# Token rows gathered as half rows into both partition halves, and turned by identity products in opposite corners of the array

## The chip, the cores and the metric

The kernel runs on one core of one Trainium2 chip. Its time is the device time of one execution in microseconds (us). The core has five engines that run on their own and wait for each other by semaphores: TensorE (PE in the rows; PEld is its weight loads), VectorE (DVE), ScalarE (ACT), GpSimd (POOL) and SyncE (SP). Transfers between device memory (HBM) and on-chip memory (SBUF) are issued by SP, ACT and POOL and carried by the core's 16 DMA engines. TensorE writes its products to PSUM.

## What is computed

One inference step of a two-layer decoder trunk on 520 token rows of 1024 fp32 values (512 of a prompt, 8 single-token samples). Layer 0 mixes with a gated short convolution, layer 1 with an RG-LRU recurrence. Each mixer is followed by a LayerNorm, a mixture of experts, and a second LayerNorm. Only the mixture of experts matters here:

```python
def hier_moe(x, w_group, w_expert, w_gate, w_up, w_down):   # 4 groups x 8 experts
    g = argmax(x2 @ w_group)                  # one group for each token
    vals, idx = lax.top_k(ep, TOP_K)          # two experts of the 8 in that group
    ...
    def expert_block(args):                   # xb: the rows of the tokens of expert e
        xb, e = args
        hmid = jax.nn.silu(xb @ w_gate[e]) * (xb @ w_up[e])     # 1024 -> 512
        return hmid @ w_down[e]                                 # 512 -> 1024
    ...
    y = jax.ops.segment_sum(y_rows, tok_s, num_segments=t)
```

Each of the 32 experts has three weight matrices of 2 MB in fp32, so a layer reads 201 MB of expert weights, and 520 tokens with two experts each give 32.5 rows for an expert on average.

## The kernel before

**Stages.** Mixer of layer 0, its LayerNorm and routing (0 to 279 us of the profiled execution), experts of layer 0 (to about 780), second LayerNorm and the mixer of layer 1, its norm and routing (to 1041), experts of layer 1 (to about 1548), last norm and output.

**Weights.** `ring` has nine slots of 16 KB in each partition, and each weight matrix of an expert takes one slot. SP issues their transfers in order (`expert`, L352 to L357), each after a wait on `freed` (`room`) until TensorE has used the matrix that was in the slot nine units before. The first three experts of a layer are loaded during the mixer. TensorE releases slots in this order: the down matrix of the last expert with the first product of the next expert, the gate matrix with the last product of `project(0)`, the up matrix with the first instruction of `turn_rows`.

**Rows of an expert.** LayerNorm's rows lie in HBM (`x1_dram`, 520 rows of 4 KB). DVE works out which token stands in which of an expert's 48 places and writes these numbers to `idx` (L1335); GpSimd gathers them with one indirect DMA (`gather`, L480 to L488) into `xg[e % 3]`, a buffer of 48 used partitions by 1024 values. Places without a token are out of bounds and move nothing. Three gathers are issued at once, each later one when TensorE has turned the rows that lay in its buffer (`t_mm`).

**Turning.** Products need the 1024 features on the partitions, so TensorE turns the rows (`turn_rows`, L772 to L778): eight transposes of 64 rows by 128 features into one PSUM bank. DVE scales and shifts them into `xgT` (`turned_rows`, L1388 to L1393).

**An expert** on TensorE (`expert`, L812 to L830): `project(0)` and `project(1)` are the gate and up products, each in two 64-column halves of the array; behind them stands `turn_rows` for the next expert, then `turn_hidden` when DVE has written the hidden values (L1396), then `down`. In the first expert of a layer `overflow_rows` (L761) stands between `turn_rows` and `turn_hidden`: with its result DVE writes the places of the output rows (L1379 to L1385) before it comes to the hidden values. Output rows go back to HBM by two indirect DMAs of half rows each (`scatter`, L492), from partitions 0 to 47 and 64 to 111.

**Ahead of the first expert** TensorE runs 12 products for warming (`warm(WARM)`, L571) while the first rows are gathered, then waits on `gath` and turns them.

Of the kernel before, what the change touches and what calls it, by code (L numbers as in the profile page):

```python
# [7 lines left out]
I32 = mybir.dt.int32  # L8
ALU = mybir.AluOpType
# [4 lines left out]
D = 1024  # L14
# [3 lines left out]
T = SEQ + DEC  # L18
TT = 104
NT = T // TT  # L20
# [10 lines left out]
NE = GROUPS * EPG  # L31
# [4 lines left out]
ROWS = 64  # L36
CAP = 48
OVER = T * TOPK // CAP
# [65 lines left out]
def build(nc, a, outs):  # L104
    y_prompt, y_sample, na_p, na_s, nb_p, nb_s, nh_p, nh_s = outs
    with ExitStack() as ctx:
        def sb(name, shape, dt=F32):
            return ctx.enter_context(nc.sbuf_tensor(name, shape, dt))
# [9 lines left out]
        rows_dram = nc.dram_tensor("yrows", [T, TOPK, D], F32).ap()  # L118
        half_rows = rows_dram.rearrange("t k (h n) -> (t k h) n", h=2)
# [24 lines left out]
        idx = sb("idx", [CAP, NBLK], I32)  # L144
        cur = sb("cur", [CAP, 3], I32)
# [68 lines left out]
        xg = [A[:ROWS, i * D:(i + 1) * D] for i in range(UNROLL)]  # L214
# [224 lines left out]
        def _(pool):  # L439
# [25 lines left out]
            pool.iota(tokid[:, :], pattern=[[TT, NT]], base=-NOROW, channel_multiplier=1,  # L465
# [8 lines left out]
            for l in L:  # L474
# [6 lines left out]
                def gather(e):  # L481
                    if e >= UNROLL:
                        pool.wait_ge(t_mm[l], e - UNROLL + 1)
                    pool.indirect_dma_start(  # L484
                        out=xg[e % UNROLL][:CAP], out_offset=None, in_=x1_dram[l],
                        in_offset=bass.IndirectOffsetOnAxis(ap=idx[:, e:e + 1], axis=0),
                        bounds_check=T - 1, oob_is_err=False,
                    ).then_inc(gath[UNROLL * l + e % UNROLL], 16)  # L488
# [9 lines left out]
                for e in range(NE + UNROLL + 1):  # L498
                    if e < NE:
                        gather(e)  # L500
                    if e == UNROLL + 1:
                        pool.wait_ge(idx_ok[l], 2)
                    if e > UNROLL:
                        d = e - UNROLL - 1
                        pool.wait_ge(y_act[l], d + 1)
                        scatter(yo[d % UNROLL], lambda nh: dest[:, nh, d:d + 1], y_out[d % UNROLL])
                n_over = pool.value_load(over_i[0:1, OVER:OVER + 1], min_val=0, max_val=OVER)
                with pool.If(n_over > 0):
                    pool.wait_ge(t_mm[l], NE)

                    def settle(j):

                        pool.tensor_tensor(unused[:, 2 * l + j:2 * l + j + 1], half_neg[:, :1], half_neg[:, :1],
                                           ALU.mult).then_inc(v_cur[l], 1)

                    with pool.Fori(0, n_over) as o:
                        pool.tensor_copy(cur[:, 0:1], idx[:, bass.ds(o + NE, 1)]).then_inc(v_cur[l], 1)
                        pool.tensor_copy(cur[:, 1:2], dest[:, 0, bass.ds(o + NE, 1)]).then_inc(v_cur[l], 1)
                        pool.tensor_copy(cur[:, 2:3], dest[:, 1, bass.ds(o + NE, 1)]).then_inc(v_cur[l], 1)
                        pool.wait_ge(v_cur[l], o * 5 + 3)  # L520
                        settle(0)
                        pool.indirect_dma_start(
                            out=xg[0][:CAP], out_offset=None, in_=x1_dram[l],
                            in_offset=bass.IndirectOffsetOnAxis(ap=cur[:, 0:1], axis=0),
                            bounds_check=T - 1, oob_is_err=False,
                        ).then_inc(v_gath[l], 16)
                        pool.wait_ge(v_ya[l], o + 1)
                        settle(1)
                        scatter(yo[0], lambda nh: cur[:, 1 + nh:2 + nh], v_out[l])
                        pool.wait_ge(v_out[l], o * 32 + 32)  # L530
                    pool.wait_ge(over_done[l], 1)
# [11 lines left out]
        def _(pe):  # L543
# [93 lines left out]
            for l in L:  # L637
# [134 lines left out]
                def turn_rows(x, done, free=False):  # L772
                    xv = x.rearrange("r (p k) -> r k p", k=KT)
                    for k in range(KT):
                        mm = pe.transpose(ps[:, 0, k * ROWS:(k + 1) * ROWS], xv[:, k, :], ident[:ROWS, :ROWS])  # L775
                        if free and k == 0:
                            mm.then_inc(freed, 1)
                    mm.then_inc(done, 1)  # L778
# [30 lines left out]
                def expert(e, e0, trip=0, more=True, first=False):  # L809
# [8 lines left out]
                    if more:  # L818
                        pe.wait_ge(gath[UNROLL * l + b], 16 * ((e0 + 1) // UNROLL + 1) + trip * 16)
# [13 lines left out]
                pe.wait_ge(gath[UNROLL * l], 16)  # L833
# [10 lines left out]
                with pe.If(n_over > 0):  # L844
# [4 lines left out]
                    with pe.Fori(0, n_over) as o:  # L849
                        pe.wait_ge(v_gath[l], o * 16 + 16)  # L850
# [239 lines left out]
        def _(dve):  # L1090
# [89 lines left out]
            for l in L:  # L1180
# [154 lines left out]
                tsc(idx[:, :NE], ps[:CAP, 5, :NE], float(NOROW), ALU.add).then_inc(idx_ok[l], 1)  # L1335
# [22 lines left out]
                def overflow():  # L1358
# [158 lines left out]
```

## Time and profile before

| | |
|---|---|
| Time, median of three runs | 1599.68 us (1595.18 to 1599.91) |
| Profiled execution, its own time | 1603.98 us |
| Its span | 1601.9 us |
| Mean granted TensorE clock | 0.943 |
| TensorE matmul busy | 1300.0 us (81%) |
| DVE, ACT, POOL busy | 395.9, 202.2, 205.9 us |
| HBM read and written | 459.53 MB, 19.19 MB |

Busy time of TensorE is no bound by itself, since the ends of its pipelined products are modelled. The stretches matter more: in the expert stages the DMA engines are busy nearly all the time; in the mixers they are not. The time outside the span is 2.1 us.

### The profile page before, as it was taken

The numbers are of one execution on the slowest core, as the hardware profiler recorded it, in microseconds if no ns is written. First come the engines' busy times: TensorE is split into PE (matmuls) and PEld (weight loads), VectorE is DVE, ScalarE is ACT, GpSimd is POOL, SyncE is SP. The second block draws the span as 40 slices with busy tenths as digits, with TensorE's granted clock in tenths as the row PEclk, the third lists the DMA queues.
The fourth block names the chain that finished last, engine by engine and source line by source line (L and its number), as shares of the span: only waits on it lengthen the run. The fifth ranks groups of instructions, "written<-read, shape, count | busy, mean of one in ns | idle before, by whom it ended". The sixth has DMA issues, their size and how long they took to land.

```text
span 1601.9 us, 19565 instructions
## 1 busy us (share of the span) xinstructions
PE 1300.0 (81%) x8158; PEld 884.9 (55%) x8158; DVE 395.9 (25%) x809; ACT 202.2 (13%) x318; POOL 205.9 (13%) x228
## 2 busy tenths in 40 slices
PE   8999998999777787778369999799887787777850
PEld 7888876565444444444158887656444444444420
DVE  1211214431111111111145663443111111111116
ACT  1000011000000000000044652200000000000002
POOL 0000001122111111111010000112211111111104
PEclk8999998899999999999779999889999999999985
DMA  9922204799999999999793202469999999999954
GB/s 236 303 105 105 106 1 167 257 399 403 404 409 409 399 410 405 410 399 407 240 293 150 82 29 102 163 252 375 403 406 397 406 412 392 412 395 401 417 182 119
DMA packets 109162, 471.18 MB, mean 294 GB/s; under 512 B 14391, under 2 KB 49207, under 8 KB 91684
## 3 DMA queue, kind: packets, MB, share of 16 engines
q1 hardware_dynamic: 93324, 443.09, 72.2%
q0 software_dynamic: 10240, 17.06, 3.2%
q10 hardware_dynamic: 5552, 10.39, 2.3%
q8 instruction: 32, 0.52, 0.1%
q14 instruction: 14, 0.11, 0.0%
HBM read 459.53 MB, written 19.19 MB: 299 GB/s over the span
## 4 chain that ended last, share of the span: by engine, by line
PE 40%; DMA 29%; SPq 24%; DVE 3%; issue 2%; POOL 1%; ACT 1%; POOLq 0%; DVEq 0%; ACTq 0%
SPq L357 23%; PE ps L547 18%; DMA ring<-in_moe_w_gate 14%; PE ps L785 8%; PE ps L631 7%; DMA ring<-in_moe_w_up 6%; DMA ring<-in_moe_w_down 4%; PE ps L804 4%; DMA Bt<-yrows 1%; DMA ring<-yrows 1%; DMA ring<-in_a_w_in 1%; PE ps L775 1%; PE ps L649 1%; PE ps L683 1%; PE ps L571 1%
## 5 line engine op out<-in xcount | busy, mean ns | idle before, releaser
L785 PE MATMUL ps<-ring,A 128*64 128x256 f32 x4096 | 487.5, 393 | 144.7 <-DMA ring<-in_moe_w_up 97.2
L785 PEld LDWEIGHTS ps<-ring,A 128*64 128x64 f32 x4096 | 320.4, 142 | 332.8 <-issue 135.6
L547 PE MATMUL ps<-A,ring 128*128 128x260 f32 x1280 | 286.2, 386 | 2.5 <-DMA ring<-in_a_w_in 2.5
L804 PE MATMUL ps<-ring,C 128*64 128x512 f32 x1024 | 239.1, 609 | 40.1 <-DMA ring<-in_moe_w_down 15.8
L547 PEld LDWEIGHTS ps<-A,ring 128*128 128x128 f32 x1280 | 245.6, 192 | 41.0 <-issue 2.7
L1396 DVE TENSOR_TENSOR C<-C,ps 128x256 f32<-128x256 f32 x64 | 26.9, 420 | 769.9 <-ACT C L1017 769.9
L804 PEld LDWEIGHTS ps<-ring,C 128*64 128x64 f32 x1024 | 79.1, 139 | 159.3 <-issue 137.7
L484 POOL DMA_INDIRECT A<-x,idx x64 | 61.2, 957 | 487.1 <-PE ps L775 458.3
L631 PE MATMUL ps<-Bt,ring 128*128 128x260 f32 x512 | 116.1, 385 | 1.0 <-ACT C L942 0.8
L631 PEld LDWEIGHTS ps<-Bt,ring 128*128 128x128 f32 x512 | 96.1, 190 | 20.1 <-DVE A L1244 2.5
L1017 ACT ACTIVATE C<-ps 128x256 f32<-128x256 f32 x64 | 24.6, 384 | 569.3 <-PE ps L785 569.2
L775 PEld LDWEIGHTS ps<-ident,A 64*128 64x128 f32 x512 | 61.2, 200 | 24.1 <-issue 23.8
L775 PE MATMUL ps<-ident,A 64*128 64x64 f32 x512 | 70.0, 277 | 0.0
L476 POOL TENSOR_TENSOR stat<-stat,half_neg 104x5 f32<-104x5 f32 x2 | 2.4, 1188 | 462.3 <-DVE stat L1100 462.3
L492 POOL DMA_INDIRECT yrows<-A,Bt x44 | 39.4, 895 | 141.0 <-ACT A L1022 127.7
L492 POOL DMA_INDIRECT yrows<-Bt x44 | 39.9, 907 | 133.2 <-ACT Bt L1022 126.5
L492 POOL DMA_INDIRECT yrows<-C,Bt x40 | 37.4, 934 | 109.6 <-ACT C L1022 103.5
L1393 DVE TENSOR_TENSOR A<-A,gb 128x512 f32<-128x512 f32 x64 | 44.3, 692 | 2.2
L1390 DVE TENSOR_TENSOR A<-ps,gb 128x512 f32<-128x512 f32 x64 | 43.5, 680 | 3.5 <-PE ps L775 3.5
L563 PE MATMUL ps<-ident,C 104*128 104x104 f32 x80 | 13.8, 347 | 36.0 <-ACT C L1056 33.6
L1399 DVE COPY C<-ps 128x256 f32<-128x256 f32 x64 | 27.2, 424 | 36.8 <-PE ps L794 36.8
L1244 DVE SCALAR_TENSOR_TENSOR A<-A,ps 128x520 f32<-128x520 f32 x16 | 11.1, 696 | 90.4 <-PE ps L631 90.4
(210 smaller groups left out, 662.2 us busy)
## 6 DMA issues: line engine op xcount, KB each, us to landing
ring<-in_moe_w_gate SPq DMA_DIRECT2D x64, 2048.0 KB
ring<-in_moe_w_up SPq DMA_DIRECT2D x64, 2048.0 KB
ring<-in_moe_w_down SPq DMA_DIRECT2D x64, 2048.0 KB
ring<-in_a_w_in SPq DMA_DIRECT2D x24, 512.0 KB, 17.8
ring<-in_b_w_in SPq DMA_DIRECT2D x8, 1024.0 KB
ring<-yrows SPq DMA_DIRECT2D x8, 832.0 KB
x<-C ACTq DMA_DIRECT2D x10, 416.0 KB
ring<-in_a_w_out SPq DMA_DIRECT2D x2, 2048.0 KB
```

The costliest lines, as they stand in the source:

```text
L357: sp.dma_start(out, w[l][e]).then_inc(loaded[s], 16)
L484: pool.indirect_dma_start(out=xg[e % UNROLL][:CAP], out_offset=None, in_=x1_dram[l], in_offset=bass.IndirectOffsetOnAxis(ap=idx[:, e:e + 1 ...
L492: pool.indirect_dma_start(out=half_rows, out_offset=bass.IndirectOffsetOnAxis(ap=where(nh), axis=0), in_=rows[nh * ROWS:nh * ROWS + CAP, : ...
L547: mm = pe.matmul(bank, lhs(k), rhs(k), start=(k == 0), stop=(k == KT - 1))
L631: mm = pe.matmul(ps[:, 2 * PAIR[m] + hf, :HALF], ring[:, s, col:col + P], hT[:, k, hf * HALF:(hf + 1) * HALF], start=(k == 0), stop=(k == ...
L775: mm = pe.transpose(ps[:, 0, k * ROWS:(k + 1) * ROWS], xv[:, k, :], ident[:ROWS, :ROWS])
L785: mm = pe.matmul(ps[hf * ROWS:(hf + 1) * ROWS, 1, u * FH:(u + 1) * FH], xgT[:, k, :], ring[:, slot, col:col + FH], start=(k == 0), stop=(k ...
L804: mm = pe.matmul(ps[nh * ROWS:(nh + 1) * ROWS, 2, :], hidT[:, at:at + ROWS], ring[:, slot, m * D + nh * 512:m * D + (nh + 1) * 512], start ...
L1390: tt(xgT, ps[:, 0, :KT * ROWS].rearrange("p (k t) -> p k t", k=KT), gb[:, 2 * l, :].unsqueeze(2).broadcast_to([P, KT, ROWS]), ALU.mult).th ...
L1393: tt(xgT, xgT, gb[:, 2 * l + 1, :].unsqueeze(2).broadcast_to([P, KT, ROWS]), ALU.add).then_inc(ready, 1)
L1396: tt(gated, gated, ps[:, 1, FH:2 * FH], ALU.mult).then_inc(ready, 1)
L1399: dve.tensor_copy(hidT, ps[:, 4, :FT * ROWS]).then_inc(ready, 1)
```

## The change

`xg[i]` becomes 128 partitions by 512 values: partition 0 to 47 hold features 0 to 511 of the 48 places, partition 64 to 111 features 512 to 1023. `gather` issues two indirect DMAs of 48 half rows (2 KB) from `half_x1`, the same rows seen as 1040 half rows, with indices `2t` and `2t + 1`. DVE writes both sets of indices, which now lie in `A` instead of a buffer of their own. `turn_rows` makes sixteen ordinary products with a 64 by 64 identity instead of eight transposes: eight with rows 0 to 63 and columns 0 to 63 of the array, eight with rows 64 to 127 and columns 64 to 127, taking turns, all into PSUM bank 0. The waits on `gath` count 32 for a gather instead of 16. The same is done in the overflow loops, which run only if an expert has more than 48 rows.

```diff
-        xg = [A[:ROWS, i * D:(i + 1) * D] for i in range(UNROLL)]
+        half_x1 = [x.rearrange("t (h n) -> (t h) n", h=2) for x in x1_dram]
+        xg = [A[:, i * 512:(i + 1) * 512] for i in range(UNROLL)]
+        idx = A[:CAP, UNROLL * 512:UNROLL * 512 + 2 * NBLK].bitcast(I32).rearrange("p (h b) -> p h b", h=2)
...
-                def gather(e):
-                    if e >= UNROLL:
-                        pool.wait_ge(t_mm[l], e - UNROLL + 1)
-                    pool.indirect_dma_start(
-                        out=xg[e % UNROLL][:CAP], out_offset=None, in_=x1_dram[l],
-                        in_offset=bass.IndirectOffsetOnAxis(ap=idx[:, e:e + 1], axis=0),
-                        bounds_check=T - 1, oob_is_err=False,
-                    ).then_inc(gath[UNROLL * l + e % UNROLL], 16)
+                def gather(rows, where, done):
+                    for h in range(2):
+                        pool.indirect_dma_start(
+                            out=rows[h * ROWS:h * ROWS + CAP, :], out_offset=None, in_=half_x1[l],
+                            in_offset=bass.IndirectOffsetOnAxis(ap=where(h), axis=0),
+                            bounds_check=2 * T - 1, oob_is_err=False,
+                        ).then_inc(done, 16)
...
                     for k in range(KT):
-                        mm = pe.transpose(ps[:, 0, k * ROWS:(k + 1) * ROWS], xv[:, k, :], ident[:ROWS, :ROWS])
-                        if free and k == 0:
-                            mm.then_inc(freed, 1)
+                        for h in range(2):
+                            r = slice(h * ROWS, (h + 1) * ROWS)
+                            mm = pe.matmul(ps[r, 0, k * ROWS:(k + 1) * ROWS], xv[r, k, :], ident[r, r], start=True, stop=True)
+                            if free and k == 0 and h == 0:
+                                mm.then_inc(freed, 1)
...
-                tsc(idx[:, :NE], ps[:CAP, 5, :NE], float(NOROW), ALU.add).then_inc(idx_ok[l], 1)
+                for h in range(2):
+                    ins = tsc(idx[:, h, :NE], ps[:CAP, 5, :NE], float(NOROW + h), ALU.add)
+                ins.then_inc(idx_ok[l], 1)
...
-                    tsc(idx[:, NE:], ps[:CAP, 5, 128:128 + OVER], float(NOROW), ALU.add)
                     for nh in range(2):
+                        tsc(idx[:, nh, NE:], ps[:CAP, 5, 128:128 + OVER], float(NOROW + nh), ALU.add)
```

On GpSimd, at the start of layer 0's experts (`A<-x_0` is a gather, `yrows<-` a scatter), these stood before:

```order
L484 DMA A<-x_0,idx 48x1024 [waits idx_ok0,turned1,x1_out]
L484 DMA A<-x_0,idx 48x1024 x2
L484 DMA A<-x_0,idx 48x1024 [waits t_mm0] x2
L492 DMA yrows<-A,Bt 2080x512 [waits y_act0,idx_ok0]
L492 DMA yrows<-A,Bt 2080x512
```

and these stand there now:

```order
L484 DMA A<-x_0,A 48x512 [waits idx_ok0,turned1,x1_out]
L484 DMA A<-x_0,A 48x512 x5
L484 DMA A<-x_0,A 48x512 [waits t_mm0]
L484 DMA A<-x_0,A 48x512
L484 DMA A<-x_0,A 48x512 [waits t_mm0]
L484 DMA A<-x_0,A 48x512
L492 DMA yrows<-A,Bt 2080x512 [waits y_act0,idx_ok0]
```

Each gather is two DMAs in a row, and nothing else changed its place.

On TensorE, from the warming products to the first overflow product of layer 0, these stood before:

```order
L571 MATMUL ps<-ident 128x128 x12
L775 MATMUL ps<-ident,A 128x64 [waits gath0_0]
L775 MATMUL ps<-ident,A 128x64 x7
L785 MATMUL ps<-ring,A 64x256 [waits loaded1,t_sb0]
L785 MATMUL ps<-ring,A 64x256 x15
L785 MATMUL ps<-ring,A 64x256 [waits gath0_1,loaded2]
L785 MATMUL ps<-ring,A 64x256 x15
L775 MATMUL ps<-ident,A 128x64 x8
L761 MATMUL ps<-Bt 48x32 [waits hot_ok]
```

and these stand there now:

```order
L569 MATMUL ps<-ident 128x128 x12
L775 MATMUL ps<-ident,A 64x64 [waits gath0_0]
L775 MATMUL ps<-ident,A 64x64 x15
L785 MATMUL ps<-ring,A 64x256 [waits loaded1,t_sb0]
L785 MATMUL ps<-ring,A 64x256 x15
L785 MATMUL ps<-ring,A 64x256 [waits gath0_1,loaded2]
L785 MATMUL ps<-ring,A 64x256 x15
L775 MATMUL ps<-ident,A 64x64 x16
L759 MATMUL ps<-Bt 48x32 [waits hot_ok]
```

Eight transposes with 128 output partitions have become sixteen products with 64, at the same two places. An ordinary fp32 product in such a list can be two instructions in the trace.

## Rows read from the trace of the kernel before

**Rows 1.** The page: what the DMA engines moved, in 40 slices of the span.
```profile
GB/s 236 303 105 105 106 1 167 257 399 403 404 409 409 399 410 405 410 399 407 240 293 150 82 29 102 163 252 375 403 406 397 406 412 392 412 395 401 417 182 119
```
**Rows 2.** Experts of layer 0 by windows: length; busy (instructions) of each engine; clock, DMA share, GB/s.
```profile
340.00:760.00 420.00, 337.18 (x2417) 197.11 (x2414) 55.70 (x105) 26.49 (x54) 71.05 (x78) 0.98 1.01 405
```
**Rows 3.** The page: groups of instructions.
```profile
L785 PE MATMUL ps<-ring,A 128*64 128x256 f32 x4096 | 487.5, 393 | 144.7 <-DMA ring<-in_moe_w_up 97.2
L775 PE MATMUL ps<-ident,A 64*128 64x64 f32 x512 | 70.0, 277 | 0.0
```
**Rows 4.** Chain that ended last, around the first expert of layer 0.
```profile
274.55 4.84 PE ps L571 x24
279.39 1.04 PE ps L775 x8
...
282.00 8.81 PE ps L785 x64
291.83 2.82 PE ps L761 x60
297.06 6.35 PE ps L804 x16
303.40 6.91 PE ps L785 x64
312.27 3.65 PE ps L804 x16
```
**Rows 5.** Timeline of the start of layer 0's experts.
```profile
274.66 0.18 DVE L1100 TENSOR_SCALAR idx<-ps 48x32 int32<-48x32 f32 x1 [0.83 <-PE ps L754]
...
275.86 1.16 POOL L484 DMA_INDIRECT A<-x,idx  x1 [13.70 <-DVE idx L1100]
...
277.32 0.94 POOL L484 DMA_INDIRECT A<-x,idx  x1 [0.30 <-issue]
```
**Rows 6.** DMA of 274 to 282 us: GB/s in 40 slices of 0.2 us.
```profile
GB/s 0 0 82 0 0 0 0 0 0 0 0 0 0 41 0 0 0 0 144 102 123 205 82 0 103 143 82 266 164 21 41 225 123 225 143 0 0 0 0 0
```
**Rows 7.** DMA of 1036 to 1044 us, likewise.
```profile
GB/s 0 0 0 0 0 0 0 0 0 0 0 0 0 0 0 0 0 164 61 184 225 62 0 0 103 82 41 143 21 0 82 123 41 246 41 0 0 0 0 0
```
**Rows 8.** Timeline of the start of layer 1's experts.
```profile
1040.91 1.09 PE L775 MATMUL ps<-ident,A 64*128 64x64 f32 x8
```
**Rows 9.** Timeline of the first expert of layer 0.
```profile
287.57 0.35 SPq L357 DMA_DIRECT2D ring<-in_moe_w_gate  x1
...
290.74 1.09 PE L775 MATMUL ps<-ident,A 64*128 64x64 f32 x8
...
294.85 0.44 DVE L1100 TENSOR_SCALAR Bt<-ps 48x32 int32<-48x32 f32 x4
...
295.35 0.40 DVE L1396 TENSOR_TENSOR C<-C,ps 128x256 f32<-128x256 f32 x1
...
303.85 0.39 SPq L357 DMA_DIRECT2D ring<-in_moe_w_down  x1
```
**Rows 10.** Windows of 2 us there: PE busy, clock, DMA share, GB/s.
```profile
282.00:284.00 2.00, 2.00 (x10) 0.51 0.17 47
...
300.00:302.00 2.00, 2.00 (x6) 0.50 0.02 8
```
**Rows 11.** Windows of 1 us around one gather in mid-stage: POOL busy, clock, DMA share, GB/s.
```profile
517.00:518.00 1.00, 0.94 (x1) 1.00 1.06 451
...
521.00:522.00 1.00, 0.00 (x0) 1.00 1.15 369
522.00:523.00 1.00, 0.34 (x1) 1.00 0.96 270
523.00:524.00 1.00, 0.69 (x2) 1.00 0.98 320
```
**Rows 12.** The page: DMA queues, packets, MB, share of 16 engines.
```profile
q1 hardware_dynamic: 93324, 443.09, 72.2%
q0 software_dynamic: 10240, 17.06, 3.2%
```

More of the change, by code:

```diff
@@ L143, in build @@
         wts = sb("wts", [TT, TOPK * NT])
-        idx = sb("idx", [CAP, NBLK], I32)
-        cur = sb("cur", [CAP, 3], I32)
+        cur = sb("cur", [CAP, 4], I32)
         over_i = sb("over_i", [1, OVER + 1], I32)
@@ L464, in _ @@
                       allow_small_or_imprecise_dtypes=True).then_inc(consts, 1)
-            pool.iota(tokid[:, :], pattern=[[TT, NT]], base=-NOROW, channel_multiplier=1,
+            pool.iota(tokid[:, :], pattern=[[2 * TT, NT]], base=-NOROW, channel_multiplier=2,
                       allow_small_or_imprecise_dtypes=True).then_inc(consts, 1)
@@ L499, in _ @@
                     if e < NE:
-                        gather(e)
+                        if e >= UNROLL:
+                            pool.wait_ge(t_mm[l], e - UNROLL + 1)
+                        gather(xg[e % UNROLL], lambda h: idx[:, h, e:e + 1], gath[UNROLL * l + e % UNROLL])
                     if e == UNROLL + 1:
@@ L516, in _ @@
                     with pool.Fori(0, n_over) as o:
[L517 to L520, printed above, removed]
+                        for h in range(2):
+                            pool.tensor_copy(cur[:, h:h + 1], idx[:, h, bass.ds(o + NE, 1)]).then_inc(v_cur[l], 1)
+                            pool.tensor_copy(cur[:, 2 + h:3 + h], dest[:, h, bass.ds(o + NE, 1)]).then_inc(v_cur[l], 1)
+                        pool.wait_ge(v_cur[l], o * 6 + 4)
                         settle(0)
[L522 to L526, printed above, removed]
+                        gather(xg[0], lambda h: cur[:, h:h + 1], v_gath[l])
                         pool.wait_ge(v_ya[l], o + 1)
                         settle(1)
-                        scatter(yo[0], lambda nh: cur[:, 1 + nh:2 + nh], v_out[l])
+                        scatter(yo[0], lambda nh: cur[:, 2 + nh:3 + nh], v_out[l])
                         pool.wait_ge(v_out[l], o * 32 + 32)
@@ L818, in expert @@
                     if more:
-                        pe.wait_ge(gath[UNROLL * l + b], 16 * ((e0 + 1) // UNROLL + 1) + trip * 16)
+                        pe.wait_ge(gath[UNROLL * l + b], 32 * ((e0 + 1) // UNROLL + 1) + trip * 32)
                     project(1, slots[1], False).then_inc(gu_mm[l], 1)
@@ L832, in _ @@
                 warm(WARM)
-                pe.wait_ge(gath[UNROLL * l], 16)
+                pe.wait_ge(gath[UNROLL * l], 32)
                 turn_rows(xg[0], t_mm[l])
@@ L849, in _ @@
                     with pe.Fori(0, n_over) as o:
-                        pe.wait_ge(v_gath[l], o * 16 + 16)
+                        pe.wait_ge(v_gath[l], o * 32 + 32)
                         pe.matmul(ps[:ROWS, 1, :ROWS], ident[:, :ROWS], ident[:, :ROWS], start=True, stop=True)
@@ L1334, in _ @@
                 dve.wait_ge(idx_mm, 3 * l + 1)
-                tsc(idx[:, :NE], ps[:CAP, 5, :NE], float(NOROW), ALU.add).then_inc(idx_ok[l], 1)
+                for h in range(2):
+                    ins = tsc(idx[:, h, :NE], ps[:CAP, 5, :NE], float(NOROW + h), ALU.add)
+                ins.then_inc(idx_ok[l], 1)
                 for k in range(TOPK):
```

## The prediction

> **What bounds the kernel now.** I read the page's slices first, then windows over the expert stages, then the chain, and last the two starts of an expert stage in the timeline.
>
> The slices of what the DMA engines moved show two plateaus at about 400 GB/s, and these are the expert stages [rows 1]. The window over layer 0's has the DMA engines busy at 1.01 of their time and 405 GB/s, with TensorE busy 337 of 420 us [rows 2]; TensorE's longest waits there are for weights [rows 3]. So from some point on, an expert stage ends when its 201 MB have come, and what TensorE, DVE or GpSimd spend on an expert counts only as far as it changes the transfers.
>
> Where is that point? A slot of the ring comes free only when TensorE uses its matrix. At the start all nine slots are full and nothing moves until the first gate product has ended: SP issues the first gate transfer at 287.57, and the next down transfer at 303.85, when the second expert begins [rows 9]. Between 300 and 302 the engines move 8 GB/s [rows 10]: they have run dry. After 303.85 an expert takes TensorE about 12.5 us (303.40 to 315.9, the end of the next `down` [rows 4]) and three matrices of 2 MB take the DMA engines 6.29 MB / 405 GB/s = 15.5 us, so the backlog only grows. The consequence for all that follows: a microsecond lost or won on the way to 303.85 moves the end of the stage by one, in each layer, and a microsecond of TensorE after it moves nothing. In the saturated part (29 experts of a layer, of whose gathers about 27 are issued in it, 54 in both layers) only a change in what the DMA engines deliver counts.
>
> **The change part by part, ahead of the second expert.**
>
> *The first gather.* Today GpSimd starts it at 275.86 and the second at 277.32 [rows 5]. The transfers stand in the slices: the first from 277.6 to 278.6, the second from 278.8 to 280.0 [rows 6]; in layer 1, 1039.4 to 1040.4 and 1040.8 to 1042.0 [rows 7]. TensorE turns the first rows at 279.39, when the 12 warming products are through [rows 4], and at 1040.91 [rows 8]: 0.8 and 0.5 us after the last bytes. The gather is just hidden. After the change the second DMA carries the other half of the same rows and comes where the second gather comes now, 1.4 us after the first. Ahead of it DVE makes one more conversion of 0.18 us [rows 5]. Last bytes then at about 280.2 and 1042.2. If the semaphore needs nothing, that is 0.8 and 1.3 us after today's turn; if it needs all of the 0.5 us, 1.3 and 1.8. A half gather moves half the bytes, and its slices may shrink from 1.2 us to about 0.6. I take 0.9 + 1.3 = 2.2 us for both layers, with bounds of 0.5 and 3.1. TensorE has nothing else to do there: behind the waiting turn stand DVE's two passes and then every product.
>
> The Trainium skill ("DMA: Bandwidth & Descriptors", Rules for kernel authors) says of two transfers to disjoint halves of the partitions that they serialize, and advises one transfer. By that rule the second half comes after the first; today's two gathers, one behind the other in [rows 6], agree.
>
> *The turn.* Eight transposes take 1.09 us [rows 9], eight instructions in the trace (512 for 64 experts [rows 3]). Fp32 products are two instructions each (4096 for 64 experts of 32 products [rows 3]), so sixteen become 32. No row shows a 64 by 64 product. Nearest below: the gate and up products run in two halves of the array at 6.91 us for 64 with 256 columns [rows 4], 0.42 ns a column, so 27 ns for 64 columns if both corners run at once, 32 x 27 = 0.9 us and some 0.2 us for the last to end: no loss. Nearest in size: the overflow products, 48 weight columns, 2.82 us for 60 [rows 4], 47 ns each; 32 x 47 + 0.2 = 1.7 us. Above: the same stretched from 48 to 64 weight columns, 63 ns, 2.2 us. I take the middle, since it is the shortest spacing that any fp32 product shows: +0.6 us for a turn.
>
> Two turns of a layer lie ahead of 303.85: that of expert 0, and that of expert 1 at 290.74, behind which the overflow products start at 291.83 and DVE's places, the hidden values and `down` wait [rows 4, 9]. Four in all: +2.4 us, bounds 0 and +4.5. The other 60 turns lie in the saturated part; with cover gone they would cost 36 us.
>
> The Trainium skill ("TensorEngine Tiling (Array Packing)", Restrictions and Gotchas) says that different row tiles cannot access one PSUM bank at the same time, and both corners write bank 0. By that rule the corners take turns and the upper value holds, 4 x 1.1 = 4.5 us in place of 2.4; no row of this kernel has two row tiles, so none shows it.
>
> *DVE.* The block of conversions behind the overflow products (four of them 0.44 us [rows 9]) gets one more, 0.11 us, ahead of the hidden values: 0.2 us in both layers.
>
> **In the saturated part.** The bytes stay the same, the gathers' DMAs go from 64 to 128. The queues' own shares give a price: 51.3 us for 10240 packets of 1.67 KB on queue 0, 1157 us for 93324 of 4.75 KB on queue 1 [rows 12], or with 16 engines 80 and 198 ns a packet. A line through both has 16 ns for a packet of no bytes. Queue 0 has 53 packets for each of its 192 DMAs; 64 more DMAs are 3400 packets, 3.4 us in all. Some will be hidden, and short rows may be packed: I take 1 us, bounds 0 and 3.4.
>
> There is a second, larger cost that the page doesn't show. One gather in mid-stage is issued at 517, and four to seven microseconds later the engines, still busy, deliver 369, 270 and 320 GB/s [rows 11], against 405 over the stage: (36 + 135 + 85) / 405 = 0.6 us lost. Over 54 gathers this is 34 us. What the change makes of it no row tells: bytes and rows stay the same, pieces are half as long, and they go to twice the partitions in two portions. I take no change, with bounds of 15 us less and 15 us more, since neither reason excludes a gain or a loss.
>
> GpSimd spends 0.94 us more on a gather, 60 us in all, and is busy 71 of 420 us [rows 2]; each gather is issued three experts ahead. Nothing waits for that.
>
> **Sum.** 2.2 + 2.4 + 0.2 + 1.0 = +5.8 us on the profiled execution's 1603.98 us, so 1609.8. That execution is 4.3 us above the median of the three runs; carried to the median, 1599.68 + 5.8 = 1605.5.
>
> **The rivals.**
>
> *The gather's dip shrinks (faster).* If the dip comes from all 4 KB rows going to 48 partitions, twice the partitions at half the bytes each relieve it. Place: every gather in the saturated part. It decides from 0.2 us a gather on: 54 x 0.2 = 11 us against the 5.8. A third to a half of 0.6 us saved is 11 to 17 us: 1588 to 1595. For it: the dip stands at the gather, and the engines are still busy in it, so something there makes the bytes slow [rows 11]. Against: the two halves come one after the other, so at any moment as many bytes go to as few partitions as today. 0.20.
>
> *The dip grows (clearly slower).* If it belongs to each piece or each indirect DMA, twice as many cost up to twice as much: a quarter to a half more is 54 x 0.15 to 0.3 = 8 to 16 us, 1613 to 1621. 0.14.
>
> *The start costs nothing.* The corners run at once, the half gathers land as soon as the whole one, or TensorE's clock, at 0.51 when the first products start [rows 10], stays up: `project(0)` and `project(1)` of the first expert take 8.81 us, the second's 6.91, and `down` 6.35 against 3.65 [rows 4]. The first of these differences, 1.9 us a layer, could go if the turn keeps TensorE busy up to the products; waiting longer for the gather could as well enlarge it. Then 1597 to 1602, no measurable change. 0.18.
>
> *The forecast*: start costs 3 to 8 us, dips stay: 1602 to 1610. 0.48.
>
> **How the numbers follow.** A measurement of this kernel tells 0.3%, 4.8 us, from no change, so slower begins at 1604.5. About two thirds of the forecast case lie above it (0.32), with the growing dip 0.46. Faster, below 1594.9: most of the first rival, and a little of luck at the start, 0.21. The rest, 0.33, is no change. The range leaves out the outer part of both dips: 1590 to 1616. The likeliest case's own is 1602 to 1610.
>
> **What the changed profile would show.** Right: at both starts the first turn begins about 1 us after the warming products end, its releaser a DMA; a turn spans about 1.7 us in 32 instructions; the down transfer of 303.85 is issued 2 to 3 us later counted from the write of the indices; 405 GB/s in mid-stage, and dips of the same depth. Wrong: a mid-stage rate off by 1% (4 GB/s), since that alone is 9 us; a turn of 1.1 or 2.2 us; clock rows at the starts that differ from today's.

## The result, and the profile after

The changed kernel takes 1613.9 us (median of 4 runs, 1612.95 to 1615.89) against 1599.2 us for the kernel before beside it (1595.18 to 1599.91, 4 runs): ratio 1.0099, 95% interval [1.0079, 1.0119], slower by some 15 us. I had forecast 1605.5. Sign and place were right. The size was not, +5.8 us in the sum and +14.7 measured, and most of what is missing comes from waits that the sum did not have.

The page of the changed kernel: groups of instructions and the queues, as in [rows 3, 12].

```profile
L484 POOL DMA_INDIRECT A<-x,A x128 | 122.5, 957 | 504.6 <-PE ps L775 450.1
L775 PE MATMUL ps<-ident,A 64*64 64x64 f32 x2048 | 136.8, 284 | 3.9 <-DMA A<-x,A 3.9
q1 hardware_dynamic: 93324, 443.09, 71.9%
q0 software_dynamic: 12288, 17.07, 3.1%
```

128 gathers and 2048 product instructions, as counted ahead. The products are busy 136.8 us where the transposes were 70.0. Queue 0 has 2048 packets more, not 3400, and no larger share.

Windows over the expert stages of both layers: the first as in [rows 2].

```profile
340.00:760.00 420.00, 364.89 (x3070) 228.10 (x3066) 58.11 (x109) 26.50 (x54) 97.14 (x105) 0.98 1.01 404
1120.00:1500.00 380.00, 327.49 (x2723) 201.70 (x2721) 51.25 (x96) 23.55 (x48) 88.84 (x95) 0.97 1.01 402
```

TensorE has 28 us more work in the first window and GpSimd 26, and the DMA engines still deliver 404 GB/s against 405 (402 against 403 in layer 1). From the issue of the first down transfer to that of the last, the stages take 437.4 and 441.1 us, against 437.3 and 442.5 before. The saturated part didn't pay.

So the time must lie in the starts. Timeline of the changed kernel at the start of layer 0's experts, to be read beside [rows 5, 9].

```profile
274.87 0.28 DVE L1100 TENSOR_SCALAR A<-ps 48x32 int32<-48x32 f32 x2 [0.82 <-PE ps L752]
...
276.16 1.16 POOL L484 DMA_INDIRECT A<-x,A  x1 [13.80 <-DVE A L1100]
...
280.19 2.14 PE L775 MATMUL ps<-ident,A 64*64 64x64 f32 x32 [0.39 <-DMA A<-x,A]
281.35 0.93 POOL L484 DMA_INDIRECT A<-x,A  x1 [0.31 <-issue]
282.59 0.93 POOL L484 DMA_INDIRECT A<-x,A  x1 [0.30 <-issue]
284.84 0.69 DVE L1392 TENSOR_TENSOR A<-ps,gb 128x512 f32<-128x512 f32 x1 [5.96 <-remote]
...
294.92 2.13 PE L775 MATMUL ps<-ident,A 64*64 64x64 f32 x32
...
296.99 2.88 PE L759 MATMUL ps<-Bt 104*48 104x32 f32 x60
...
299.08 0.93 POOL L484 DMA_INDIRECT A<-x,A  x1 [0.30 <-issue]
300.87 0.17 DVE L1100 TENSOR_SCALAR A<-ps 48x21 int32<-48x21 f32 x1 [9.73 <-PE ps L759]
...
308.98 0.39 SPq L358 DMA_DIRECT2D ring<-in_moe_w_down  x1
```

Two things stand out. The turn is over at 282.33 by its records, but VectorE gets its result at 284.84; it had followed within 0.11 us of the end before. And the overflow products end at 299.87 and VectorE goes on at 300.87, a wait of 1.00 us, where it was 0.11. The two lines of the kernel before, to be read behind the turn of [rows 4] and the overflow products, which ended at 294.64:

```profile
280.52 0.69 DVE L1390 TENSOR_TENSOR A<-ps,gb 128x512 f32<-128x512 f32 x1 [1.96 <-PE ps L775]
...
294.75 0.17 DVE L1100 TENSOR_SCALAR idx<-ps 48x21 int32<-48x21 f32 x1 [7.92 <-PE ps L761]
```

The report of the turn is late for both engines that wait for it: GpSimd's next gather, held by the same count, starts 0.67 us after VectorE's pass before (281.19) and after (285.51).

The same place in layer 1.

```profile
1040.23 0.28 DVE L1100 TENSOR_SCALAR A<-ps 48x32 int32<-48x32 f32 x2 [0.82 <-PE ps L752]
1044.40 1.02 POOL L484 DMA_INDIRECT A<-x,A  x1 [15.90 <-issue]
...
1048.30 2.19 PE L775 MATMUL ps<-ident,A 64*64 64x64 f32 x32 [3.50 <-DMA A<-x,A]
...
1052.97 0.69 DVE L1392 TENSOR_TENSOR A<-ps,gb 128x512 f32<-128x512 f32 x1 [8.73 <-remote]
```

Here GpSimd also starts its first gather 4.17 us behind the write of the indices, and "issue" says that nothing in the profile held it. In the kernel before it was 1.09 us:

```profile
1036.63 0.18 DVE L1100 TENSOR_SCALAR idx<-ps 48x32 int32<-48x32 f32 x1 [0.82 <-PE ps L754]
...
1037.72 1.02 POOL L484 DMA_INDIRECT A<-x,idx  x1 [13.90 <-DVE idx L1100]
```

From the write of the indices to the first down transfer, the start takes in us (each from its own timeline):

| kernel | layer 0 | layer 1 | median time |
|---|---|---|---|
| before | 29.2 | 28.5 | 1598.3 to 1599.2 |
| changed | 34.1 | 36.6 | 1613.9 |
| half gathers alone (e4) | 30.4 | 32.6 | 1601.7 |
| later gathers held (e7) | 30.5 | 36.2 | 1609.1 |
| four gathers in a row (e15) | 33.6 | 36.1 | 1610.6 |
| eight in a row (e14) | 38.5 | 36.8 | 1623.0 |
| places later, on before (e9) | 23.8 | 22.8 | 1597.4 |

The changed kernel's starts are 4.9 and 8.1 us longer, 13.0 us in all, and the difference of the medians is 14.7 (12.6 to 19.0). The two profiled executions themselves are only 9.1 us apart in span, 1601.9 and 1611.0: beside the 13.0 of the starts, the other stretches are 3.9 us shorter in the changed one. So the starts carry the loss, but the trace doesn't account for the 14.7 to the microsecond.

### The profile page after: what moved, and what is told of

It is laid out like the page before. It is cut to its first block, busy times and chain, and to the rows that moved or that the text cites. A ratio compares the mean times of both kernels' runs of the same rounds, so it can differ in the third digit from the quotient of the medians.

```text
span 1611.0 us, 22769 instructions
## 1 busy us (share of the span) xinstructions
PE 1360.1 (84%) x9694; PEld 952.8 (59%) x9694; DVE 396.4 (25%) x813; ACT 202.3 (13%) x318; POOL 269.2 (17%) x292
## 4 chain that ended last, share of the span: by engine, by line
PE 45%; SPq 24%; DMA 24%; DVE 3%; issue 2%; another core or an unknown queue 1%; POOL 1%; ACT 1%; POOLq 0%; DVEq 0%; ACTq 0%
SPq L358 23%; PE ps L545 18%; DMA ring<-in_moe_w_up 12%; PE ps L785 9%; PE ps L629 7%; PE ps L804 5%; DMA ring<-in_moe_w_down 4%; DMA ring<-in_moe_w_gate 3%; PE ps L775 2%; DMA Bt<-yrows 1%; DMA ring<-yrows 1%; DMA ring<-in_a_w_in 1%; PE ps L647 1%; PE ps L681 1%
## 5 line engine op out<-in xcount | busy, mean ns | idle before, releaser
L785 PEld LDWEIGHTS ps<-ring,A 128*64 128x64 f32 x4096 | 323.8, 141 | 268.1 <-issue 116.3
L484 POOL DMA_INDIRECT A<-x,A x128 | 122.5, 957 | 504.6 <-PE ps L775 450.1
L775 PEld LDWEIGHTS ps<-ident,A 64*64 64x64 f32 x2048 | 127.9, 212 | 28.1 <-issue 23.8
L775 PE MATMUL ps<-ident,A 64*64 64x64 f32 x2048 | 136.8, 284 | 3.9 <-DMA A<-x,A 3.9
L1392 DVE TENSOR_TENSOR A<-ps,gb 128x512 f32<-128x512 f32 x64 | 43.6, 681 | 14.7 <-remote 14.7
L561 PE MATMUL ps<-ident,C 104*128 104x104 f32 x80 | 12.7, 326 | 37.4 <-ACT C L1056 33.7
L561 PEld LDWEIGHTS ps<-ident,C 104*128 104x128 f32 x80 | 10.5, 184 | 40.0 <-ACT C L1056 35.6
```

The lines of the kernel that those rows point to most:

```text
L484: pool.indirect_dma_start(out=rows[h * ROWS:h * ROWS + CAP, :], out_offset=None, in_=half_x1[l], in_offset=bass.IndirectOffsetOnAxis(ap=wh ...
L775: mm = pe.matmul(ps[r, 0, k * ROWS:(k + 1) * ROWS], xv[r, k, :], ident[r, r], start=True, stop=True)
L785: mm = pe.matmul(ps[hf * ROWS:(hf + 1) * ROWS, 1, u * FH:(u + 1) * FH], xgT[:, k, :], ring[:, slot, col:col + FH], start=(k == 0), stop=(k ...
L1392: tt(xgT, ps[:, 0, :KT * ROWS].rearrange("p (k t) -> p k t", k=KT), gb[:, 2 * l, :].unsqueeze(2).broadcast_to([P, KT, ROWS]), ALU.mult).th ...
```

## The experiments

**A report that comes late because nothing follows?** If TensorE reports a turn late because nothing stands behind it, work behind it brings the report forward.

```diff
                 turn_rows(xg[0], t_mm[l])
+                warm(2)
```

> The changed kernel, with two warming products (they need no data and write a spare bank) right behind the first turn of each layer. Theory 'the last product of a turn reports late when nothing follows it': DVE starts 2.3 to 2.6 us after the turn's first instruction instead of 4.6, in both layers, and the kernel gains about 4 us (2.3 us a layer, less 0.2 for the two products) against the changed one. Rival 'the first use of the corners is slow': DVE still starts 4.6 us after it, and nothing is gained.

1612.7 us, ratio 1.0085 [1.0056, 1.0115]. Timeline of this kernel, layer 0.

```profile
280.06 2.14 PE L775 MATMUL ps<-ident,A 64*64 64x64 f32 x32 [0.52 <-DMA A<-x,A]
...
282.12 0.71 PE L569 MATMUL ps<-ident 128*128 128x128 f32 x4
282.50 0.93 POOL L484 DMA_INDIRECT A<-x,A  x1 [0.30 <-issue]
284.73 0.69 DVE L1393 TENSOR_TENSOR A<-ps,gb 128x512 f32<-128x512 f32 x1 [5.94 <-remote]
```

TensorE is through the turn and at the next products at 282.12, and VectorE still waits until 284.73. So by the records it isn't the turn that is slow; what comes late is what tells VectorE of it. The theory is refuted: the release is 4.67 us behind the turn's start, as without the two products.

**The corners one after the other.**

```diff
-                    for k in range(KT):
-                        for h in range(2):
-                            r = slice(h * ROWS, (h + 1) * ROWS)
+                    for h in range(2):
+                        r = slice(h * ROWS, (h + 1) * ROWS)
+                        for k in range(KT):
```

> The changed kernel, with the eight products of the first corner ahead of the eight of the second instead of taking turns. Theory 'the 32 instructions follow each other at 62 ns whatever corner they are in': a turn still spans 2.1 us and DVE's wait behind turn_hidden in mid-stage stays 1.6 us; no change in time. Rival 'changing corner costs': a turn takes under 1.7 us. Rival 'the corners overlap at least in part': a turn takes over 2.6 us once they no longer alternate.

1666.6 us, ratio 1.042 [1.0392, 1.0448]. **And products in place of the transposes, in the kernel before**, rows in 48 partitions as ever:

```diff
-mm = pe.transpose(ps[:, 0, k * ROWS:(k + 1) * ROWS], xv[:, k, :], ident[:ROWS, :ROWS])
+mm = pe.matmul(ps[:, 0, k * ROWS:(k + 1) * ROWS], xv[:, k, :], ident[:ROWS, :ROWS], start=True, stop=True)
```

> The kernel before, with its eight transposes replaced by eight fp32 products with the same identity (64 rows by 128 features, 16 instructions); gathers as before. Theory 'a product is two instructions, each as long as a transpose's': a turn spans 1.9 to 2.1 us against 1.09, four turns ahead of the point where transfers saturate, so 3 to 4 us slower than before and nothing in mid-stage. If the late report of a last instruction belongs to products at large, the first turn of a layer ends 4.6 us after its start here too; if it belongs to corners, it does not. Rival 'turns are hidden': within 1 us of before.

1705.0 us, ratio 1.0654 [1.0625, 1.0684]. A turn in mid-stage and the window of 340 to 760, first corner by corner, then products of 128 columns.

```profile
515.65 3.62 PE L775 MATMUL ps<-ident,A 64*64 64x64 f32 x32
```
```profile
340.00:760.00 420.00, 403.82 (x2907) 263.66 (x2906) 58.90 (x105) 25.13 (x51) 95.72 (x102) 0.91 1.00 401
```
```profile
507.48 4.01 PE L775 MATMUL ps<-ident,A 64*128 64x64 f32 x16
```
```profile
340.00:760.00 420.00, 404.09 (x2406) 256.37 (x2408) 60.03 (x105) 24.12 (x49) 68.38 (x75) 0.90 0.97 385
```

3.62 us for 32 instructions is 113 ns each, 4.01 for 16 is 250, and the changed kernel's alternating corners take 2.13 for 32, 67 ns. So the turn's products go by their weight columns (64 or 128), 1.8 to 2 ns each, and taking turns between the corners hides much of it. The columns alone don't set the time: the overflow products take 2.88 us for 60 instructions of 48 columns, 48 ns, 1 ns a column. Their weights lie side by side and the turn's lie eight values apart, but no run separates the two. The Trainium skill ("TensorEngine Tiling (Array Packing)", Restrictions and Gotchas) says that row tiles cannot access one PSUM bank at the same time. Both corners write bank 0 here, and alternating gains all the same, 67 against 113 ns. The value that the prediction drew from the rule, 4.5 us for four turns, nearly came out, 4.2; that the bank is the reason isn't shown. Whether they ever write it at one moment the runs don't tell: weight loads of one corner beside products of the other would gain too. The first turn of a layer in the kernel that goes corner by corner tells something else: it takes 3.67 us, and VectorE is released 4.63 us behind its start, 1.30 behind the last of the six gathers, just as with a turn of 2.14. The plain products release it 0.11 us behind a turn of 4.06, with three gathers in a row.

I had expected no change or little from the first kernel, and 3 to 4 us from the second; it is 53 us against the changed kernel and 106 against the one before. The windows show why: with 1.5 or 1.9 us more for a turn than in the changed kernel, TensorE, busy 404 of 420 us at a clock of 0.9, becomes what an expert takes, and the DMA engines are no longer full in the second kernel. So the slack that hides the longer turns in the saturated part is real, but 1.5 us more an expert use it up, with the lower clock that comes with it.

**Half gathers alone.** The kernel before with each gather in two, half rows side by side in the same 48 partitions; transposes as before.

```diff
...
+ for h in range(2):
      pool.indirect_dma_start(
-         out=xg[e % UNROLL][:CAP], out_offset=None, in_=x1_dram[l],
+         out=rows[:CAP, h * 512:(h + 1) * 512], out_offset=None, in_=half_x1[l],
...
```

> The kernel before, with only the gathers changed: two indirect DMAs of half rows each, side by side into the same 48 partitions; eight transposes as before. Theory 'half rows cost only the wait at the start and one instruction fetch': first turn 0.7 us later after the indices are written in layer 0, in layer 1 0.7 us or, if GpSimd's code fetch falls ahead of the first gather as in the changed kernel, 3 to 4 us; 403 to 405 GB/s in mid-stage; 1.5 to 5 us slower than before. Rival 'the dip at each gather grows': 400 GB/s or less in mid-stage and over 8 us slower.

1601.7 us, ratio 1.0018 [1.0003, 1.0032]. Timeline of this kernel: the first release in layer 0, the overflow products behind the second turn, and the first gather of layer 1.

```profile
282.01 0.93 POOL L484 DMA_INDIRECT A<-x,A  x1 [0.30 <-issue]
282.07 0.69 DVE L1390 TENSOR_TENSOR A<-ps,gb 128x512 f32<-128x512 f32 x1 [2.52 <-issue]
...
293.31 2.88 PE L759 MATMUL ps<-Bt 104*48 104x32 f32 x60
...
295.38 0.93 POOL L484 DMA_INDIRECT A<-x,Bt  x1 [0.30 <-issue]
297.15 0.17 DVE L1098 TENSOR_SCALAR A<-ps 48x21 int32<-48x21 f32 x1 [8.77 <-PE ps L759]
...
1038.94 1.02 POOL L484 DMA_INDIRECT A<-x,A  x1 [15.90 <-issue]
```

Its starts are 1.2 and 4.1 us longer, and it has three of the costs: the gather lands later, the 4.2 us ahead of layer 1's first gather (indices at 1034.76), and the wait behind the overflow products (they end at 296.19 and VectorE goes on at 297.15). It doesn't have the fourth: the first turn's result is taken within 0.11 us, in both layers, though the fifth of GpSimd's six gathers starts just then. The Trainium skill ("SBUF — State Buffer", SBUF: two separate sides) describes a port pair that GpSimd's instructions and some kinds of VectorE's hold exclusively, the other waiting for the whole instruction. Here VectorE's pass starts 0.06 us after a gather has started, and in the changed kernel the pass waits on for 1.3 us when no gather is being issued any more, so such a lock isn't what keeps it waiting.

**GpSimd's code moved, first attempt.** Twelve `pool.nop()` ahead of the layers, in the changed kernel.

> The changed kernel, with twelve empty instructions on GpSimd near its start, so that everything behind them lies twelve places further on in its code. Theory 'in layer 1 GpSimd's first gather waits 3 us for a piece of its code': the first gather of layer 1 starts 1.0 us after the indices are written instead of 4.2 (the fetch falls in an earlier wait), and the stage of layer 1 starts 3 us sooner. Rival 'it waits for the rows written to HBM': still 4.2 us.

1614.0 us, ratio 1.0092 [1.0074, 1.011], and 4.18 us ahead of layer 1's gather. It tells nothing of the theory: the idle instructions do not stand in the built program, so it is the changed kernel once more, and its time and starts (33.7 and 36.5 us) come out the same.

**Later gathers held behind the first turn.**

```diff
-                        if e >= UNROLL:
-                            pool.wait_ge(t_mm[l], e - UNROLL + 1)
+                        if e >= UNROLL or e == 1:
+                            pool.wait_ge(t_mm[l], max(1, e - UNROLL + 1))
```

> The changed kernel, with the gathers of a layer's experts 1 and 2 issued only when the first turn is done. Theory 'the first turn takes 4.6 us and not 2.1 because four gathers run beside it': DVE starts 2.2 us after the turn's start in layer 0 and in layer 1, 2.4 us a layer won, some 5 us in all. Rival 'it is slow for another reason (first use of the corners, or TensorE idle before it)': 4.6 us as before, no gain.

1609.1 us, ratio 1.0057 [1.004, 1.0073]: 4.8 us back. Timeline and one window of this kernel, layer 0; then the window at the same place in layer 1.

```profile
280.21 2.13 PE L775 MATMUL ps<-ident,A 64*64 64x64 f32 x32 [0.61 <-DMA A<-x,A]
282.46 0.69 DVE L1392 TENSOR_TENSOR A<-ps,gb 128x512 f32<-128x512 f32 x1 [3.64 <-PE ps L775]
...
283.94 7.13 PE L785 MATMUL ps<-ring,A 128*64 128x256 f32 x64 [1.59 <-DVE A L1395]
```
```profile
284.00:288.00 4.00, 4.00 (x38) 2.70 (x40) 3.69 (x14) 0.00 (x0) 3.03 (x4) 1.00 0.22 58
1048.00:1052.00 4.00, 3.71 (x18) 2.19 (x20) 3.69 (x15) 0.00 (x0) 3.08 (x4) 0.50 0.12 29
```

VectorE is released 0.1 us behind the end of the turn in both layers (282.46 and 1046.81, turns over at 282.34 and 1046.70), 2.4 us sooner after its start. In layer 0 the clock stays at 1.00 and the products take 7.13 us in place of 8.68. In layer 1 it stands at 0.50, they take 9.79 in place of 8.62, and `down` is longer too: the start is only 0.4 us shorter there, against 3.6 in layer 0.

**The corners used ahead of the turn**, in place of four warming products, in case the first use is dear.

```diff
-                warm(WARM)
+                warm(WARM - 4)
+                for _ in range(4):
+                    for h in range(2):
+                        r = slice(h * ROWS, (h + 1) * ROWS)
+                        pe.matmul(ps[r, 3, :ROWS], ident[r, r], ident[r, r], start=True, stop=True)
```

> The changed kernel, with the last four warming products replaced by eight 64 by 64 products in the two corners, ahead of the wait for the rows. Theory 'the first use of the corners after full-size products is slow': the turn behind them takes 2.2 us instead of 4.6. Rivals 'gathers beside it' or 'idle before it': 4.6 us still.

1616.1 us, ratio 1.0104 [1.0087, 1.0121], VectorE released 4.61 and 4.55 us behind the turn's start. Refuted.

**How many gathers in a row.** Two more gathers of 64 bytes a row behind the six, and in another kernel the third expert's held, so that four are left.

```diff
                         gather(xg[e % UNROLL], lambda h: idx[:, h, e:e + 1], gath[UNROLL * l + e % UNROLL])
+                        if e == 2:
+                            for h in range(2):
+                                pool.indirect_dma_start(
+                                    out=xtra[:, 2 * l + h, :], out_offset=None, in_=small[l],
...
```

> The changed kernel with two more gathers behind the six at the start of each layer: they bring 16 numbers a row into a spare tile that nothing reads, so they add hardly any traffic but keep GpSimd issuing for 2.5 us longer. In the four kernels in which six gathers stand in a row, VectorE was released by the first turn 1.26 to 1.36 us behind the end of the last gather, whatever the turn itself took. Theory A (the report of the first turn waits for the end of GpSimd's row of gathers): VectorE starts 7.1 us behind the start of the first turn in place of 4.65, and the time rises by about 5 us to 1619. Theory B (the turn is slowed by the traffic or by a fixed 2.4 us whenever gathers run beside it): VectorE still starts 4.6 us behind the turn and the time rises by under 1 us.

```diff
-                        if e >= UNROLL:
-                            pool.wait_ge(t_mm[l], e - UNROLL + 1)
+                        if e >= UNROLL or e == 2:
+                            pool.wait_ge(t_mm[l], max(1, e - UNROLL + 1))
```

> The changed kernel with the gathers of the third expert held until the first turn is done, so that four stand in a row at the start of a layer and not six. The fourth would be issued about as the first turn starts and end 0.85 us behind that. Theory A (the report waits for the end of the row, and 1.3 us more): VectorE starts 2.2 us behind the turn, as with two gathers in a row, and the time is that of the kernel with all later gathers held, 1609. Theory B (any gather beside the turn slows it by about the same): 4.6 us and 1614. In between, some 3.4 us, would speak for a cost for each gather that is in flight beside the turn.

Timeline of the kernel with eight in a row, both layers.

```profile
280.77 2.13 PE L787 MATMUL ps<-ident,A 64*64 64x64 f32 x32 [1.33 <-DMA A<-x,A]
...
285.63 0.93 POOL L510 DMA_INDIRECT xtra<-x,A  x1 [0.30 <-issue]
288.27 0.69 DVE L1404 TENSOR_TENSOR A<-ps,gb 128x512 f32<-128x512 f32 x1 [8.84 <-remote]
...
1047.00 1.02 POOL L487 DMA_INDIRECT A<-x,A  x1 [13.09 <-DMA x<-C]
...
1051.00 2.14 PE L787 MATMUL ps<-ident,A 64*64 64x64 f32 x32 [0.77 <-DMA A<-x,A]
```

And of the one with four.

```profile
280.44 0.93 POOL L484 DMA_INDIRECT A<-x,A  x1 [0.31 <-issue]
280.51 2.14 PE L775 MATMUL ps<-ident,A 64*64 64x64 f32 x32 [0.34 <-DMA A<-x,A]
282.77 0.69 DVE L1392 TENSOR_TENSOR A<-ps,gb 128x512 f32<-128x512 f32 x1 [3.56 <-PE ps L775]
```

Eight: 1623.0 us, ratio 1.0154 [1.0124, 1.0185]; VectorE is released 7.5 us behind the turn's start in both layers, 1.7 to 1.8 behind the end of the last gather. Four: released after 2.26 us; 1610.6 us, ratio 1.0076 [1.0051, 1.0102]. With six it is 4.65, 1.3 behind the last gather's end. The tiny gathers add next to no bytes, so it is the row of gathers that sets the time of the release, not the bytes. Whether it is the end of their issue on GpSimd or the landing of their data isn't separated: with six, the last packets land at about 284.6 and VectorE is released at 284.84; with eight, at about 287.6 and 288.27. The first pair beyond the turn's own does no harm by itself: it is issued by 281.37, and 1.3 us on is the end of the turn. The time of the eight rose by 9 us, but its two starts by only 4.5; the rest is spread over the other stretches, and I haven't explained it. The four keep less than they gain at the turn, since the clock is low again: their products take 9.91 us.

**GpSimd's code moved, with instructions that exist**, on top of the held gathers: 16 tiny products into spare columns.

```diff
+            for i in range(16):
+                pool.tensor_tensor(unused[:, 2 * DEPTH + i:2 * DEPTH + i + 1], half_neg[:, :1], half_neg[:, :1], ALU.mult)
```

> The changed kernel with its fourth and later gathers of each layer (those of the second expert on) held until the first turn is done, and 16 small GpSimd products (they write spare columns, nothing reads them) placed ahead of the layers, so that all GpSimd code behind them stands 16 instructions later. The holding alone gave 1609.1 us (ratio 1.0057). In that run layer 1's first gather still started 4.17 us behind the write of its indices, against 1.09 us in the kernel before, and the 12 idle instructions tried before do not stand in the built program at all, so they tested nothing. Theory A (a fetch of GpSimd's code falls between the write and the first gather, because of how much code lies ahead of it): the fetch moves ahead of the wait, the first gather of layer 1 starts 1.1 to 1.3 us behind the write, and the time falls by about 3 us to 1606. Theory B (the 3.1 us belong to the doubled gathers themselves, not to where their code lies): still 4.2 us and 1609.

1611.7 us, ratio 1.008 [1.0056, 1.0104], and layer 1's first gather at 1042.87, 4.15 us behind the indices. My theory A failed, at least for a shift by 16 instructions. But theory B fails too: the kernel with eight in a row has doubled gathers and starts them after 1.36 us.

**The places of the overflow blocks a block later.** First in the kernel before, then together with the held gathers and the moved code in the changed one.

```diff
-                    if first:
+                    if over:
                         overflow_rows()
...
-                    expert(e, e, first=(e == 0))
+                    expert(e, e, first=(e == 0), over=(e == 1))
```

> The kernel before (one gather, transposes), with the overflow products and the writing of the output places moved from a layer's first expert to its second, and the residual work on DVE to the third. If all that counts is what lies ahead of the second expert, its down transfer is issued 2.7 us sooner in each layer (3.5 us of work taken off, silu's table load ends 0.8 us behind the turn), up to 5.4 if down runs at full clock for being reached sooner: 5 to 10 us faster than before, and mid-stage at 405 GB/s. Rival 'the transfers make up any delay of the start': no change.

> The changed kernel with everything taken off its start that can be taken off: later gathers held behind the first turn, GpSimd's code moved by 16 instructions, and the places of the overflow blocks and of the rows to write worked out beside the second expert in place of the first (this alone made the kernel before 0.15 per cent faster, 1597.45 us). If the cost of the change lies only in the start of the expert stages, what remains against that kernel is two first turns of +1.05 us, two second turns of +1.05 us and two gathers of +0.66 us, 5.5 us in all: 1603. If something in the saturated stretch pays as well, or if the places cost as much beside the second expert as beside the first: 1606 or more.

1597.4 us, ratio 0.9985 [0.9971, 1.0]; and 1605.1 us, ratio 1.0042 [1.0025, 1.0059]. In the kernel before the starts fall to 23.8 and 22.8 us, but the second expert now carries the places and the stretch up to the last down transfer grows, from 437.3 to 440.0 and from 442.5 to 446.3: what the start wins is mostly given back. I had expected 5 to 10 us less; the starts gave 11.1 and the time 1.3. Against this kernel the changed one with all three is still 7.7 us behind, where I expected 5.5: its starts are 25.7 and 29.0 us, and in layer 1 the first gather still starts 4.5 us behind the indices. In both kernels no gather is issued while the overflow products run, and VectorE follows these 0.03 us behind their end, against 1.00 in the changed kernel. No version tried is faster than the kernel before by more than 0.3%.

## Why the prediction fell short, by its own steps

**The range and the number.** The measured 1613.9 lies within my 1590 to 1616 by luck: that width was for the dips, which did not move, and the likeliest case's 1602 to 1610 misses. The time falls where I had put the growing dip (1613 to 1621), which is not what happened. Of the signs, a turn of 2.2 us stood under wrong, and the down transfer was to be 2 to 3 us late and is 4.9 and 8.1.

**What bounds the kernel: right in the main.** The saturated part takes the same time with 28 us more of TensorE's in a window. Half gathers alone show the same (437.3 to 435.2, 442.5 to 442.6). Too strong was that a microsecond of TensorE behind the second expert's start moves nothing: with the places moved there, the stretch behind it grew by 2.7 and 3.8 us.

**The queues' 1.0 us and the dips: no change, as taken for the dips.** 404 and 402 GB/s against 405 and 403. The packets came to 2048 more and not 3400: a half gather has 32, not the 53 of the queue's mean. Both rivals on the dips fall: half the bytes to twice the partitions neither relieved nor deepened them enough to see. The 1.0 us isn't seen either.

**The first gather, +2.2 us: mis-sized in one part, blind in another.** From the start of the first gather to that of the turn it is 4.03 us against 3.46 and 3.90 against 3.19, +1.3 for both layers together. But in layer 1 the gather itself starts 3.1 us later, which no row of before showed and which I hadn't thought to ask.

**The turn, +0.6 us each: the wrong row.** It takes 1.05 us more, four times +4.2 in place of +2.4. I took the spacing of products with 48 weight columns as the middle; the bound that I had stretched to 64 columns, 2.2 us a turn, is what was measured, 2.13 to 2.19. That it fits is partly luck: one corner alone costs 113 ns an instruction, far more than the 63 stretched from the overflow products, and taking turns brings it down to 67.

**What the sum left out: how a result reaches the next engine.** I had costed instructions and transfers, and for GpSimd's 0.94 us a gather I wrote "Nothing waits for that". Something does. The first turn's result is held until the six gathers are through, +2.4 us a layer (4.65 against the 2.25 of the kernels with two and four), 4.8 in all. This wait, put at nothing, is the largest step that the prediction had wrong. Behind the overflow products the second half gather now runs to the end of the products, and 0.9 us a layer go there, 1.8 in all, with transposes as well.

**Added up:** gather 1.3, late first gather of layer 1 3.1, turns 4.2, held first results 4.8, held overflow results 1.8, VectorE's conversions 0.2 (as forecast), and the clock gives back 2.1 (`down` 5.28 and 5.35 us where it took 6.35 and 6.24, `project` 8.68 for 8.81): 13.3 us, against 13.0 in the starts. The three terms that the forecast had for the starts, 4.8 us, came to 5.7; the other 7.6 are terms that it didn't have. **The rival that the start costs nothing** is refuted. The clock did give something back, but at `down` and not at the products that it named.

**Open:** why layer 1's first gather starts late. All kernels with doubled gathers but one have it, 4.15 to 4.5 us; the one with two gathers more in layer 0 has not (1.36), and neither the hold nor 16 instructions moved it. A packet of the instruction queues lies in the gap in the changed kernel, but none in the one with the moved code. One coincidence no run has tested: VectorE is busy with a run of small instructions until 4.0 us behind the write of the indices, and in all these traces but one (4.5) the late gather starts 0.15 to 0.2 us after that run ends. In layer 0 the first gather starts in the midst of the same run. And open is what ties TensorE's report to GpSimd's gathers, and why half gathers with transposes escape it at the first turn: that the release moves with the length of the row is shown, the path isn't.

## What to carry to other kernels

An engine that "has time" isn't free if it issues indirect DMAs: look at what other engines report while it does, and keep a row of gathers from running on past the first result that everything waits for. Don't cost a small fp32 product by the spacing of another that looks like it: per weight column the overflow products and the turn's differ by nearly two, so the spacing has to be measured on the product itself. And ask of the start of a saturated stage alone whether it got longer. The kernels here then ended later, though not one for one: 13.0 us of starts and 14.7 of time, 5.3 and 2.9 with half gathers alone, and work moved from the start to the next expert was mostly paid there.

## What the runs showed of the hardware

- VectorE's release by a finished TensorE turn came 2.3 us behind the turn's start with two or four indirect DMAs in a row, 4.65 with six, 7.5 with eight. With products behind the turn, TensorE's own records went on without a gap meanwhile. With transposes of 1.09 us and six in a row it came at the turn's end.
- Fp32 products whose weights lie eight values apart, each instruction: with 64 weight columns 67 ns in two opposite corners by turns and 113 in one corner after the other, all into one PSUM bank; with 128 columns 250 ns.
- At a start the granted clock fell to 0.50 or stayed at 1.00, and 64 products of 256 columns took 7.13 to 9.91 us. The 7.13 and the 9.91 both stand behind the same wait of 1.59 us after a turn of 2.13 us, in two kernels (gathers held, four in a row), so that wait alone doesn't decide it, and no run shows what does. Holding the gathers won 2.4 us at the turn of each layer; 3.6 of the start were left in one and 0.4 in the other.
